# Experts' rows put back by one float32 product instead of two float32r products, with half of the projection's weights loaded earlier

## The reference, cut to what matters

```python
gates = jnp.sum(jax.nn.one_hot(eidx, N_EXPERTS, dtype=F32) * wsel[..., None], axis=1)

def expert_step(acc, ew):
    wg, wu, wd, gcol = ew
    h = jax.nn.silu(xt @ wg) * (xt @ wu)
    return acc + gcol[:, None] * (h @ wd).astype(F32), None
...
x = layer_norm(ALPHA * x + f, W['ln2_g'][i], W['ln2_b'][i])
gate = jax.nn.sigmoid((x @ W['w_ple_gate'][i]).astype(F32))
x = (x.astype(F32) + gate * (p[i] @ W['w_ple_proj'][i]).astype(F32)).astype(x.dtype)
```

## Time and profile before

| What | us |
|---|---|
| three runs: median, lowest, highest | 1610.71, 1609.38, 1612.32 |
| the profiled execution: own time, span of its core | 1611.03, 1609.2 |
| granted TensorE clock, mean of the span | 0.992 of 2.4 GHz |

### The profile page before, as it was taken

How to read it: one execution, slowest core, us unless ns; L and a number is a source line. 1 busy time by engine, 2 the same in 40 slices (tenths; PEclk the granted TensorE clock), 3 DMA queues, 4 the chain that set the end, 5 groups by cost and what they waited for, 6 DMA issues and landing times.

```text
span 1609.2 us, 22408 instructions
## 1 busy us (share of the span) xinstructions
PE 1562.5 (97%) x8258; PEld 793.3 (49%) x8258; DVE 537.7 (33%) x1328; ACT 339.4 (21%) x688; POOL 149.0 (9%) x241
## 2 busy tenths in 40 slices
PE   7999899999999999999999999989999999999998
PEld 5775544344444443466665754554443444444435
DVE  2157522222222222351434335462222122222226
ACT  2211122121221221221222221022211122122222
POOL 0241100000000000000111011020000000000000
PEclk9999999999999999999999999999999999999999
DMA  9733999999989999973577586589999998999990
GB/s 293 271 115 152 361 402 420 420 421 419 419 362 420 420 420 419 386 264 105 177 241 242 192 281 236 200 344 403 421 420 420 414 417 352 421 420 420 421 366 30
DMA packets 121756, 536.18 MB, mean 333 GB/s; under 512 B 17897, under 2 KB 29545, under 8 KB 73936
## 3 DMA queue, kind: packets, MB, share of 16 engines
q1 hardware_dynamic: 98599, 470.88, 73.6%
q0 software_dynamic: 21216, 61.12, 10.5%
q10 hardware_dynamic: 1872, 3.22, 0.6%
HBM read 526.15 MB, written 23.87 MB: 342 GB/s over the span
## 4 chain that ended last, share of the span: by engine, by line
PE 84%; DMA 8%; DVE 5%; issue 1%; ACT 1%; SPq 1%; DVEq 0%; POOLq 0%; ACTq 0%
PE ps L1373 24%; PE ps L1402 12%; PE ps L1157 11%; PE ps L1187 9%; DMA weights<-in_w_exp_up 7%; PE ps L1313 6%; PE ps L1366 4%; PE ps L1309 2%; PE ps L1386 2%; PE ps L1395 1%; PE ps L1066 1%; DVE x_tok L2491 1%; PE ps L1563 1%; PE ps L1330 1%; PE ps L1044 1%
## 5 line engine op out<-in xcount | busy, mean ns | idle before, releaser
L1373 PE MATMUL ps<-weights,x_feat 128*64 128x512 f32 x1856 | 408.9, 593 | 10.9 <-DMA weights<-in_w_exp_up 8.4
L1373 PEld LDWEIGHTS ps<-weights,x_feat 128*64 128x64 f32 x1856 | 134.6, 137 | 276.0 <-issue 276.0
L1402 PE MATMUL ps<-weights,arena 128*64 128x512 f32 x992 | 226.5, 599 | 0.9 <-ACT arena L1593 0.9
L1157 PE MATMUL ps<-x_feat,weights 128*128 128x288 f32 x800 | 203.6, 412 | 1.1 <-ACT x_feat L1593 1.1
L1157 PEld LDWEIGHTS ps<-x_feat,weights 128*128 128x128 f32 x800 | 154.3, 195 | 43.6 <-issue 3.8
L2247 DVE CAST split<-state 128x1024 fp32r<-128x1024 f32 (+1 forms) x66 | 44.7, 677 | 325.0 <-ACT state L1593 325.0
L2244 DVE SCALAR_TENSOR_TENSOR arena<-arena,ps 128x256 f32<-128x256 f32 x64 | 30.8, 481 | 348.7 <-ACT arena L1823 348.7
L2644 POOL DMA_INDIRECT arena<-x_rows,arena x64 | 63.6, 994 | 876.7 <-DVE arena L2237 833.4
L1593 ACT ACTIVATE state<-ps 128x512 f32<-128x512 f32 x132 | 78.8, 597 | 283.6 <-PE ps L1402 261.2
L1402 PEld LDWEIGHTS ps<-weights,arena 128*64 128x64 f32 x992 | 65.7, 136 | 132.2 <-issue 130.9
L1823 ACT ACTIVATE arena<-ps 128x256 f32<-128x256 f32 x64 | 24.5, 383 | 430.7 <-PE ps L1373 404.3
(11 more groups left out here) (311 smaller groups left out, 1323.9 us busy)
## 6 DMA issues: line engine op xcount, KB each, us to landing
weights<-in_w_exp_gate SPq DMA_DIRECT2D x124, 1024.0 KB, 13.5
weights<-in_w_exp_up SPq DMA_DIRECT2D x124, 1024.0 KB, 16.5
weights<-in_w_exp_down SPq DMA_DIRECT2D x124, 1024.0 KB, 15.0
weights<-in_w_in_c SPq DMA_DIRECT2D x24, 1024.0 KB, 7.7
arena<-in_state_ret POOLq DMA_DIRECT2D x20, 512.0 KB, 5.2
out_ret_sample<-arena POOLq DMA_DIRECT2D x20, 512.0 KB, 6.4
weights<-in_w_in_a SPq DMA_DIRECT2D x8, 1024.0 KB, 10.2
weights<-in_w_ple_gate SPq DMA_DIRECT2D x8, 1024.0 KB, 18.1
```

The source lines that it names most:

```text
L1157: last = pe.matmul(ps[:, 0:T], lhs(c), XT[:, c, :], start=(c == 0), stop=(c == n - 1))
L1373: last = pe.matmul(ps[64 * s:64 * s + 64, :], XGT[u][:, c, 64 * s:64 * s + 64], rhs, start=(c == 0), stop=(c == KC - 1))
L1402: last = pe.matmul(ps[64 * s:64 * s + 64, :], HT[u][:, c, 64 * s:64 * s + 64], wd[s][:, c, 512 * n:512 * n + 512], start=(c == 0), stop=(c ...
```

## The change

- `sums` makes one product for each (j, n) of `j = 0, 1`: `TOK`, now float32, and the unsplit rows `YF`, both plain float32.
- VectorE's `y_high` and `y_low` are gone in the loop, after it, and in the branch for overfull experts. TensorE no longer waits for `y_split`. In the loop nothing stands in its place, since the waits on banks 0 and 1 that precede `sums` already say that `YF` was written; after the last pair TensorE waits for bank 0 ahead of the first `sums` and for bank 1 ahead of the third.
- The tile `y_low` is gone. In its place stands a tile `projection` of the same size, which holds the first half of `w_ple_proj`. SP loads it at the start of the layer's expert stage, between the first half of the shared expert's down weights and the panels of the second pair. The second half stays where it was, in the `HOME` pair's place.

```diff
-        YLOW = sb("y_low", 1024, F32R)
-        TOH = sb("token_rows", 2 * T, F32R)
+        PROJb = sb("projection", 1024)
+        TOH = sb("token_rows", 2 * T)
...
-        PROJ = HOME_UP[1][:, 0:2048].rearrange("p (f n) -> p f n", f=2)
+        PROJ = PROJb[:, :], HOME_UP[1][:, 0:1024]
...
                             sp.dma_start(SHD, A["w_sh_down"][l, 0:P, :]).then_inc(sem("shared_down_in"), 16)
+                            sp.dma_start(PROJ[0], A["w_ple_proj"][l, 0:P, :]).then_inc(sem("projection_in"), 16)
...
-                for f in range(2):
-                    sp.dma_start(PROJ[:, f, :], A["w_ple_proj"][l, P * f:P * f + P, :]).then_inc(sem("projection_in"), 16)
+                sp.dma_start(PROJ[1], A["w_ple_proj"][l, P:2 * P, :]).then_inc(sem("projection_in"), 16)
...
-                    for y in (YHI, YLO):
-                        last = pe.matmul(bank((f"sum{l}", j, n)), TOK[u][:, P * j:P * j + P], y[:, 512 * n:512 * n + 512],
-                                         start=start and y is YHI, stop=stop and y is YLO, skip_group_check=True)
-                    return last
+                    return pe.matmul(bank((f"sum{l}", j, n)), TOK[u][:, P * j:P * j + P], YF[:, 512 * n:512 * n + 512],
+                                     start=start, stop=stop, skip_group_check=True)
...
                             pe.wait_ge(sem("token_onehot", l), pr)
-                            pe.wait_ge(sem("y_split", l), pr)
...
                 pe.wait_ge(sem("token_onehot", l), PAIRS)
-                pe.wait_ge(sem("y_split", l), PAIRS)
+                pe.wait_ge(bank_free[0], base[0] + LOOP_USES[0])
                 for j in range(2):
                     end(sums(j, 0, 1, True), (f"sum{l}", j, 0))
-                for b in range(3):
+                for b in range(1, 3):
                     pe.wait_ge(bank_free[b], base[b] + LOOP_USES[b])
-                pe.wait_ge(sem("y_split", l), PAIRS + 1)
                 end(sums(0, 1, 1, True), (f"sum{l}", 0, 1))
...
-                    dve.wait_ge(bank_free[0], base[0] + uses(0, pr, 2))
-                    dve.wait_ge(bank_free[1], base[1] + uses(1, pr, 2 if tail else 3))
-                    y_high().then_inc(sem("y_high", l), 1)
-                    dve.wait_ge(sem("y_high", l), pr + 1)
-                    y_low().then_inc(sem("y_split", l), 1)
```

More of the change, by code:

```diff
@@ L507, in trunk @@
         XG = [a.take(D) for _ in range(2)]
-        YHI, YLO = SPLIT[:, :], YLOW[:, :]
         TOK = [TOH[:, T * i:T * i + T] for i in range(2)]
@@ L1308, in sums @@
                         for q in range(4):
-                            last = pe.matmul(PS[TS * q:TS * q + TS, 7, 0:256], TOK[u][:, SEQ:T].bitcast(F32),
+                            last = pe.matmul(PS[TS * q:TS * q + TS, 7, 0:256], TOK[u][:, SEQ:T],
                                              YF[:, 256 * q:256 * q + 256], start=start, stop=stop, skip_group_check=True)
                         return last
-                    for y in (YHI, YLO):
-                        last = pe.matmul(bank((f"sum{l}", j, n)), TOK[u][:, P * j:P * j + P], y[:, 512 * n:512 * n + 512],
-                                         start=start and y is YHI, stop=stop and y is YLO, skip_group_check=True)
-                    return last
+                    return pe.matmul(bank((f"sum{l}", j, n)), TOK[u][:, P * j:P * j + P], YF[:, 512 * n:512 * n + 512],
+                                     start=start, stop=stop, skip_group_check=True)
                 def shared_down():
@@ L1344, in early_projection @@
                                 for q in range(4):
-                                    cols = PROJ[:, c, :].rearrange("p (n q x) -> p n q x", n=2, q=4)[:, :, q, :]
+                                    cols = PROJ[c].rearrange("p (n q x) -> p n q x", n=2, q=4)[:, :, q, :]
                                     last = pe.matmul(PS[TS * q:TS * q + TS, b, 0:256].rearrange("p (n x) -> p n x", n=2),
@@ L1348, in early_projection @@
                                 continue
-                            last = pe.matmul(PS[:, b, :], PT[:, c, o:o + r], PROJ[:, c, 512 * n:512 * n + 512],
+                            last = pe.matmul(PS[:, b, :], PT[:, c, o:o + r], PROJ[c][:, 512 * n:512 * n + 512],
                                              start=(c == 0), stop=(c == 1))
@@ L1533, in _ @@
                             down(0, 1, halves_of(last_panels[2]), PS[:, 1, :]).then_inc(sem("ov_y", l), 1)
-                            pe.wait_ge(sem("ov_yc", l), s + 1)
+                            pe.wait_ge(sem("ov_y_copied", l), s + 1)
                             for j, n in ((0, 0), (0, 1), (1, 0), (1, 1)):
@@ L1547, in project @@
                     for n in range(2):
-                        tok((f"pw{l}", j, n), lambda c: PT[:, c, o:o + r], lambda c: PROJ[:, c, 512 * n:512 * n + 512], r, 2)
+                        tok((f"pw{l}", j, n), lambda c: PT[:, c, o:o + r], lambda c: PROJ[c][:, 512 * n:512 * n + 512], r, 2)
                 def gate_logits(j, n):
@@ L2244, in hidden @@
                 return STT(HH[u], HS[u], META[u][:, 0:1], PS[:, 0, DE:2 * DE], ALU.mult, ALU.mult)
[L2246 to L2250, removed]
             base = GRP[(f"moe{l}",)]
@@ L2365, in experts_dve @@
                         hidden(0).then_inc(sem("ov_hidden", l), 1)
[L2366 to L2369, removed]
                         dve.wait_ge(sem("ov_summed", l), s + 1)
```

## The result

The changed kernel takes 1698.34 us (median of four runs, 1697.88 to 1698.93) against 1610.05 for the kernel before: a ratio of 1.0548, 95% interval 1.0534 to 1.0561, 5.5% slower. The profiled execution took 1698.73 us, 87.7 more than that of before. The prediction was 1689 us, range 1680 to 1704: the direction and the mechanism came as forecast, with 9 us missing.

A forecast was written before the change was run, and what follows sets the result against it. TensorE was taken to bound the loop, the DMA engines just behind: 1611.03 + 88.7 (longer sums) + 1.0 (layer ends) - 11.7 (ended waits) + 0.6 (early load) = 1689.6, forecast as 1689 us, range 1680 to 1704.

The forecast's parts named there:

- The price of an unsplit product: Sums of each loop pair: 0.858 us a product instead of 0.46, 1.43 us more a pair, +88.7 us over 62 pairs.
- The first rival: Sums in the loop: a plain product costs the split pair's 0.46 us, total 1607.5 us; chance 2 in 100.
- the gap at a block's start: Behind a sum block's first split record: 0.09 us for a weight load, expected to vanish beside records of 0.429 us.
- the bound with all three gaps: Upper bound for a loop pair's longer sums, keeping gaps of 0.09, 0.08 and 0.10 us: 1.59 us more a pair.
- What the DMA engines gave back: Waits before the gate and up products: eight for weights go and half of two others, -11.7 us (0 to -13.1).
- the DMA engines stay late: Rival for the loop: waits of the old size return, the 11.7 us are not given back, 1701 us; chance 8 in 100.
- they hide the longer sums: Rival for the loop: the DMA engines bind it and cover the added TensorE time, about 1611 us; chance 1 in 100.
- One sign: Expected in the changed kernel's loop: a DMA share below 0.98, where the profile before showed 1.01.
- After the last pair: Sums at each layer's end: they run without waits but end half a microsecond later, +1.0 us in all (0 to 1.6).
- The early load: 512 KB of projection weights ahead of the second pair's panels: may delay the second layer's first gather, +0.6 us (0 to 2.5).
- At no cost: VectorE's dropped split, the float32 one-hot matrix and the new waits for banks 0 and 1: no time of their own.
- Weight loads that are not hidden: Rival for the loop's sums: every record waits 0.19 us for its load, 2.95 us a pair, 1782 us; chance 1 in 100.

The follow-up runs named there:

- half-way kernel: The kernel before with only the sums of tokens 0 to 127 unsplit, VectorE still splitting and the projection loaded late: 1648.26 us, ratio 1.0230.
- doubled products: The changed kernel with every unsplit product of j = 0 and 1 issued twice: 1918.08 us in one run.
- products alone: The kernel before with unsplit plain products for j = 0 and 1, VectorE still splitting and waited for, projection loaded late: 1698.48 us, ratio 1.0547.
- high product alone: The kernel before with the low part's product left out of the sums, VectorE still computing the remainders: 1603.98 us, ratio 0.9954.

## Why the prediction came out as it did

**The price of an unsplit product** was right: four records of 594 ns in each block, 0.43 us from start to start, 0.858 us a product against 0.46 for the split pair. The first rival (a plain product costs what the split pair costs) is out by the pair of 16.13 us. The estimate on its side, 427 ns, comes from the Trainium skill's figure for FP32_LOW_HIGH (Perfetto Trace Analysis, section Engine Utilization). It fits one record, 0.429 us, and a product has two. The Trainium skill has a second page on it, FP8 and Floating Point Precision, section TensorE Precision Notes: true float32 takes four passes through the array. The trace agrees: 0.858 us a product is close to four times the 0.23 us of a float32r record.

**The step that failed is the gap at a block's start.** The prediction saw 0.09 us behind the first split record and "let this gap go", because a load of 192 ns fits beside a record of 0.429 us. But the gap was not the load's. By the starts it is the rest of the last transposes record's 0.12 us, inside which the first split record is already recorded; it belongs to the neighbour and stayed, now in front of the first record: 1.01 us instead of 0.91, 0.34 instead of 0.26. Each of a pair's eight records takes 0.20 us more, and the pair took 1.57 us more and not 1.43, near the bound with all three gaps, 1.59. Over 62 pairs that is 96.6 instead of 88.7: 7.9 of the 9 us that are missing. The first stage (+1.6) and the clock (+1.5) added 3.1 to the profiled run, and the waits gave back 1.5 more than forecast. The half-way kernel shows both kinds of front in one pair, and the doubled products show that it is paid once a block. Why the last two pairs of a layer grow by less stays open.

**What the DMA engines gave back**: the waits went, all ten instead of eight and a half; 13.2 us by the pairs' distances for -11.7 forecast. The kernel with the sums of half the tokens unsplit shows that the cause was the pair's length, and not the projection's load, which it left late. With that the rivals "the DMA engines stay late" and "they hide the longer sums" are both out. One sign did not come: the DMA share is 1.00 in the first part of the loop and not below 0.98, yet nobody waits. And the prediction put unlike things beside 420 GB/s: weights alone for the kernel before (432), weights and gathered rows for the changed one (412). Counted alike, with the rows, it is 453 and 412. The half-way kernel asks for 6.59 MB in 15.34 us, 430 GB/s, and had no wait: bytes over time against 420 did not tell where the waits begin.

**After the last pair** +0.47 us a layer for 0.5. **The early load**: 0.6 us was forecast, and the times show none (1697.05 us with it and 1698.48 for the products alone with the late load, on one chip), though up to about a microsecond could hide in the gather's scatter. **At no cost** was right for VectorE's split, by the products alone.

**Weight loads that are not hidden**: out, records came 0.43 us apart beside full loads, and the first load of a block starts with the transposes record in front of it. The gap that spoke for this rival has another source, as said.

**The sum with measured terms**: 1611.03 + 96.6 + 0.9 - 13.2 = 1695.3; the profiled run had 1.6 us more in the first stage (155.66 us against 154.06; two other runs took 154.23 and 156.61), 1.5 for the clock, and the smaller differences above. The medians of the same code were 1698.34 and 1697.05.

## What to carry to other kernels

Price an operation by starts, and ask of every gap in the timeline whose it is before letting it go. Count from a record that both kernels share, here the transposes in front: a gap behind the first record of a block can be the time of the record ahead of it, and a tenth of a microsecond twice a pair was 8 us here. Where two engines are close to binding, the same step costs most of its price in one direction (+36.6 us for half of it, 62 x 0.78 = 48 less the waits that ended) and pays little in the other (-7.7 us), so look at the second bound before taking work off the first. Work on an engine that nobody waits for can be as bulky as 123 us and still be the cheaper choice, if it keeps the busy engine's products short.

## What the runs showed of the hardware beyond that

TensorE's granted clock fell from 2.4 to 1.2 GHz behind some idle times and not behind others of the same length. In the loop of the kernel with the high product alone it fell around the idle time of 2.40 us that ended at 526.15 (8.59 instead of 7.09 us for the next 32 records), but not around 2.41 us at 298.39. At the start of the second layer's experts it fell with idle times of 1.96, 2.28, 2.52 and 2.83 us (0.52 granted behind the last), and stayed up with 1.05 to 1.68 us in six runs. A wait of some two microseconds can cost 1.5 us on top of itself, or nothing.
